# Gates read for two groups at once, twelve row sums moved from the one-hots to the second layer's groups, and three small reorderings, in a float32 transformer block pair

## The reference, cut to what matters

```
q = (xi @ w_q).reshape(n, 8, 2, 128)
s = einsum('nhpc,hpkc->nhpk', q, sub_keys)            # 128 scores on each of two sides
ts, ti = top_k(s, 16)                                 # 16 best of each side
best_s, best_p = top_k(all 256 sums of two, 16)       # 16 best pairs
gate = softmax(best_s)
act  = gelu(einsum('nd,nhkd->nhk', xi, u[idx]))
out  = einsum('nhk,nhkd->nd', gate * act, v[idx])
```

## Time and profile before

| | |
|---|---|
| time, median of 3 executions | 2229.15 us (2226.83 to 2231.83) |
| profiled execution, its own time | 2228.25 us |
| its span | 2226.9 us |
| routing (queries, key scores, u tiles, choices) | 400 to 828 us |
| one-hots | 828 to 1028 us |
| last u tiles | 1028 to about 1075 us |
| second layer's groups | about 1075 to 1590 us |
| second block | 1590 us to the end |

### The profile page before, as it was taken

One profiled execution on the slowest core, in us unless ns is written; L12 is line 12 of the kernel. 1 busy time (PEld: TensorE's weight loads), 2 busy tenths in 40 slices (PEclk: granted clock), 3 DMA queues, 4 the chain that ended last, 5 costly groups with the idle time before them and its releaser, 6 DMA issues.

```text
span 2226.9 us, 31730 instructions
## 1 busy us (share of the span) xinstructions
PE 2118.8 (95%) x12889; PEld 1230.2 (55%) x12889; DVE 1505.2 (68%) x2733; ACT 880.0 (40%) x1056; POOL 688.9 (31%) x540
## 2 busy tenths in 40 slices
PE   6999999999999989999999999999999999999998
PEld 5465665455656556666665555655645464444444
DVE  4557653798899999997788888888784374332002
ACT  5333452344334346665333333333332454434110
POOL 2421001310243332222233333334426302455440
PEclk9999999999999999999999999999999999999999
DMA  6214471215898879899999999999622201332310
GB/s 210 76 42 148 157 275 61 96 43 205 331 317 314 323 265 355 327 377 326 384 379 370 366 367 380 374 366 371 236 76 100 76 20 39 114 108 83 151 38 38
DMA packets 194482, 483.42 MB, mean 217 GB/s; under 512 B 10672, under 2 KB 93648, under 8 KB 188320
## 3 DMA queue, kind: packets, MB, share of 16 engines
q1 hardware_dynamic: 154624, 334.65, 42.0%
q0 software_dynamic: 39712, 146.74, 17.8%
HBM read 428.92 MB, written 52.43 MB: 216 GB/s over the span
## 4 chain that ended last, share of the span: by engine, by line
PE 49%; DVE 31%; DMA 13%; issue 3%; ACT 2%; POOL 1%; SPq 1%; DVEq 0%; ACTq 0%; POOLq 0%
PE psum L574 13%; PE psum L575 13%; PE psum L576 13%; DMA expert_act<-act_dram 9%; DVE weight_low L2088 7%; DVE row_sum L2336 3%; DMA rows_b<-peer_v_dram,row_index 2%; DVE rows_b L2323 2%; DVE rows_a L2323 2%; DVE hidden_low L2522 1%; POOL weight_low L2679 1%; DVE gated_one_hot_b L2502 1%; DVE one_hot_b L2499 1%; DVE one_hot_a L2496 1%; DVE expert_act L2517 1%
## 5 line engine op out<-in xcount | busy, mean ns | idle before, releaser
L574 PE MATMUL psum<-x_high,weight_high 128*128 128x384 bf16 (+3 forms) x1856 | 643.1, 346 | 16.6 <-DVE x_low L1964 5.4
L575 PE MATMUL psum<-x_low,weight_high 128*128 128x384 bf16 (+3 forms) x1856 | 642.7, 346 | 0.0
L576 PE MATMUL psum<-x_high,weight_low 128*128 128x384 bf16 (+3 forms) x1856 | 641.8, 346 | 0.0
L1348 ACT ACTIVATE weight_high<-weight_stage 128x4096 bf16<-128x4096 f32 (+2 forms) x100 | 356.2, 3563 | 260.2 <-PE psum L576 129.9
L2679 POOL TENSOR_TENSOR weight_low<-weight_stage,weight_high 128x512 bf16<-128x512 f32 (+1 forms) x229 | 296.6, 1329 | 410.4 <-ACT weight_high L1348 410.4
L574 PE MATMUL psum<-hidden_high,weight_high 128*128 128x384 bf16 x1024 | 334.5, 327 | 12.5 <-DVE hidden_low L2522 12.5
L575 PE MATMUL psum<-hidden_low,weight_high 128*128 128x384 bf16 x1024 | 334.5, 327 | 0.0
L576 PE MATMUL psum<-hidden_high,weight_low 128*128 128x384 bf16 x1024 | 334.4, 327 | 0.0
L2088 DVE TENSOR_TENSOR weight_low<-weight_stage,weight_high 128x1024 bf16<-128x1024 f32 x256 | 302.3, 1216 | 18.9 <-ACT weight_high L1348 18.8
L574 PEld LDWEIGHTS psum<-x_high,weight_high 128*128 128x128 bf16 (+1 forms) x1856 | 183.8, 99 | 169.5 <-issue 19.7
L576 PEld LDWEIGHTS psum<-x_high,weight_low 128*128 128x128 bf16 (+1 forms) x1856 | 183.8, 99 | 154.2 <-issue 6.7
(11 more groups left out here) (363 smaller groups left out, 2981.7 us busy)
## 6 DMA issues: line engine op xcount, KB each, us to landing
weight_stage<-peer_u_dram SPq DMA_DIRECT2D x32, 2048.0 KB
weight_stage<-peer_v_dram SPq DMA_DIRECT2D x32, 2048.0 KB
weight_stage<-mlp_w_dram SPq DMA_DIRECT2D x16, 2048.0 KB
weight_stage<-ada_w_dram SPq DMA_DIRECT2D x12, 2048.0 KB
act_dram<-norm_value SPq DMA_DIRECT2D x128, 192.0 KB
gate_dram<-gate_matrices SPq DMA_DIRECT2D x12, 2048.0 KB
gates<-gate_dram SPq DMA_DIRECT2D x32, 768.0 KB, 16.6
expert_act<-act_dram SPq DMA_DIRECT2D x32, 768.0 KB
```

Of the source, the lines that this page charges most:

```text
L574: self.nc.tensor.matmul(out, left[0], right[0], start=first, stop=False)
L575: self.nc.tensor.matmul(out, left[0], right[1], start=False, stop=False)
L576: return self.nc.tensor.matmul(out, left[1], right[0], start=False, stop=last)
L1348: nc.scalar.activation(k.block_view(m.w_high, n % SPLITS, n), k.block_view(m.w_stage, n % STAGES, n), ACT.Copy).then_inc(*s.w_high.up(n))
```

## The change

1. `gates` becomes twice as wide (two groups of four), and SP reads the gates of two groups in one transfer, every other group. A piece of it in memory is 1024 bytes where it was 512. The buffers are placed elsewhere so that the larger one fits.
2. `act_dram` is laid out by group, so that a group's read is one run of 6144 bytes for each partition where it was four of 1536. The 128 writes stay 128 x 1536 bytes each.
3. `ROWS_HOT` has two rows in four steps where it had three: 24 rows among the 48 steps instead of 36. `ROWS_GROUP` has 39/8 rows a group instead of 9/2, 156 instead of 144.
4. `ROUTE_ENDS` is (36, 60, 80) instead of (35, 57, 76), so 34 u tiles instead of 38 are left for the one-hots.
5. ACT's `query` takes the query first, and starts the next block's rounding one query later than before (after queries 1, 5, 9 and 13).
6. `masked` for the first two pairs comes before `small_outs` on DVE, and ACT runs one small exponential before `small_outs`.

```diff
-        m = Map(nc, top)
+        m = Map(nc, top - 512)
         self.hid_high, self.hid_low = ...
-        m = Map(nc, mats)
-        self.gates, self.act = m("gates", [P, 2, DT // TC, EG, TC]), m("expert_act", [P, 2, EG, DT])
+        self.gates = m("gates", [P, 2, DT // TC, 2 * EG, TC])
+        self.act = m("expert_act", [P, 2, EG, DT])
...
-ROUTE_ENDS = (35, 57, 76)
+ROUTE_ENDS = (36, 60, 80)
...
-ROWS_HOT = [ROWS_ROUTE[-1] + 3 * (_n + 1) // 4 for _n in range(HOT_STEPS)]
+ROWS_HOT = [ROWS_ROUTE[-1] + (_n + 1) // 2 for _n in range(HOT_STEPS)]
 ROWS_LAST = ROWS_HOT[-1] + 4
-ROWS_GROUP = [min(len(ROW_USES), ROWS_LAST + 9 * (_n + 1) // 2) for _n in range(NG)]
+ROWS_GROUP = [min(len(ROW_USES), ROWS_LAST + 39 * (_n + 1) // 8) for _n in range(NG)]
...
         def query(hp):
-            if hp % 4 == 0:
-                self.begin(("peer_q", hp // 4))
             if hp >= 2:
                 nc.scalar.wait_ge(*s.scored.at("keys", hp - 2))
             self.take(("peer_q", hp), m.query[:, hp % 2, :])
+            if hp % 4 == 1:
+                self.begin(("peer_q", hp // 4))
...
     def small_outs(self):
+        self.root_table("na", ACT.Exp)
...
         self.second_projections()
+        nc.vector.wait_ge(*s.in_window.at())
+        for p in range(2):
+            self.masked(p)
         self.small_outs()
...
-                    nc.vector.wait_ge(*s.in_gates[n % 2].at(n))
+                    nc.vector.wait_ge(*s.in_gates[n // 2 % 2].at(n // 2))
...
-            nc.sync.dma_start(k.act_dram[tile], ...)
+            nc.sync.dma_start(k.act_dram[tile // EG, :, tile % EG, :], ...)
...
         if n >= 2:
             nc.sync.wait_ge(*s.hid_low.at(n - 2, EG - 1))
-        nc.sync.dma_start(m.gates[:, n % 2, :, :, :],
-                          k.gate_dram[:, :, EG * n:EG * (n + 1), :].rearrange("c p b n -> p c b n"))...
+        if n % 2 == 0:
+            pair = n // 2
+            nc.sync.dma_start(m.gates[:, pair % 2, :, :, :],
+                              k.gate_dram[:, :, EG * n:EG * (n + 2), :].rearrange("c p b n -> p c b n"))...
-        nc.sync.dma_start(m.act[:, n % 2, :, :], k.act_dram[EG * n:EG * (n + 1)].rearrange("b p n -> p b n"))...
+        nc.sync.dma_start(m.act[:, n % 2, :, :], k.act_dram[n])...
```

More of the change, by code:

```diff
@@ L1387, in run, with root_table @@
         self.norm("final2", lambda t: s.added.at("mlp", t))
-    def root_table(self, j):
+    def root_table(self, j, func=ACT.Sqrt):
         nc, s, m = self.nc, self.s, self.m
@@ L1393, in root_table @@
             nc.scalar.wait_ge(*s.root_loaded.now())
-        nc.scalar.activation(m.root[:, 12:13], m.eps[:, 0:1], ACT.Sqrt).then_inc(*s.root_loaded.up(j))
+        nc.scalar.activation(m.root[:, 12:13], m.eps[:, 0:1], func).then_inc(*s.root_loaded.up(j))
     def norm(self, j, ready):
@@ L2514, in experts @@
                 if b == 0:
-                    nc.vector.wait_ge(*s.in_gates[n % 2].at(n))
+                    nc.vector.wait_ge(*s.in_gates[n // 2 % 2].at(n // 2))
                     nc.vector.wait_ge(*s.in_act[n % 2].at(n))
-                nc.vector.tensor_tensor(v, v, m.gates[:, n % 2, :, b, :], ALU.mult).then_inc(*s.gated.up(n, b))
+                nc.vector.tensor_tensor(v, v, m.gates[:, n // 2 % 2, :, EG * (n % 2) + b, :], ALU.mult).then_inc(*s.gated.up(n, b))
             if n < NG - 1:
@@ L2577, in small_outs, with masked @@
                                         m.x_high[:, dst + g, 0:SEQ], ALU.subtract).then_inc(*s.x_low.up(name, g))
+    def masked(self, p):
+        nc, s, m = self.nc, self.s, self.m
+        nc.vector.wait_ge(*s.in_bias[p % 2].at(p))
+        for x in range(2):
+            nc.vector.tensor_tensor(m.bias[:, p % 2, x, :, :], m.bias[:, p % 2, x, :, :], m.window[:, :, :],
+                                    ALU.add).then_inc(*s.masked.up(p, x))
     def neighbourhood(self):
         nc, s, k, m = self.nc, self.s, self.k, self.m
[L2582 to L2586, removed]
         def scores(n):
@@ L2617, in neighbourhood @@
         nc.vector.wait_ge(*s.normed.at("final1", KT - 1))
-        nc.vector.wait_ge(*s.in_window.at())
-        for p in range(2):
-            masked(p)
         n_steps = len(NA_STEPS)
@@ L2627, in neighbourhood @@
                 if t == 3 and 1 <= p < NH2 // 2 - 1:
-                    masked(p + 1)
+                    self.masked(p + 1)
                 scores(n)
@@ L2802, in fill @@
             nc.sync.wait_ge(*s.activated.at("u", tile))
-            nc.sync.dma_start(k.act_dram[tile], m.norm2.value[:, tile % 4, 0:DT]).then_inc(*s.act_spilled[tile % 4].up(tile))
+            nc.sync.dma_start(k.act_dram[tile // EG, :, tile % EG, :], m.norm2.value[:, tile % 4, 0:DT]).then_inc(*s.act_spilled[tile % 4].up(tile))
     def group(self, n):
@@ L2809, in group @@
             nc.sync.wait_ge(*s.hid_low.at(n - 2, EG - 1))
-        nc.sync.dma_start(m.gates[:, n % 2, :, :, :],
-                          k.gate_dram[:, :, EG * n:EG * (n + 1), :].rearrange("c p b n -> p c b n")).then_inc(
-            *s.in_gates[n % 2].up(n))
+        if n % 2 == 0:
+            pair = n // 2
+            nc.sync.dma_start(m.gates[:, pair % 2, :, :, :],
+                              k.gate_dram[:, :, EG * n:EG * (n + 2), :].rearrange("c p b n -> p c b n")).then_inc(
+                *s.in_gates[pair % 2].up(pair))
         for i in range(EG):
             nc.sync.wait_ge(*s.act_spilled[i].at(EG * n + i))
-        nc.sync.dma_start(m.act[:, n % 2, :, :], k.act_dram[EG * n:EG * (n + 1)].rearrange("b p n -> p b n")).then_inc(
+        nc.sync.dma_start(m.act[:, n % 2, :, :], k.act_dram[n]).then_inc(
             *s.in_act[n % 2].up(n))
@@ L2993, in build @@
     gate_dram = nc.dram_tensor("gate_dram", (DT // TC, P, NK, TC), F32, kind="Internal").ap()
-    act_dram = nc.dram_tensor("act_dram", (NK, P, DT), F32, kind="Internal").ap()
+    act_dram = nc.dram_tensor("act_dram", (NG, P, EG, DT), F32, kind="Internal").ap()
     return write(nc, dram, out, gate_dram, act_dram, reached)
```

2 lines of the change are left out of this document (1 added, 1 removed).

## The result

The changed kernel takes 2247.11 us (median of 4, 2243.23 to 2251.92), the kernel before 2227.99 on the same chip (4, 2221.72 to 2231.83). The ratio is 1.0089, interval 1.0067 to 1.0112: slower by 0.9%, where 2203 us were forecast. The profiled execution took 2251.92 us, the longest of the four, and its span is 2250.6.

What follows compares the result with a forecast made beforehand. PE was busy 95%; DVE was taken to bound the one-hots and DMA the groups. Terms -12.0 - 2.7 - 5.0 - 6.0 = -25.7 us from 2228.25 gave 2202.5, with 0.9 to the median 2203; range 2193 to 2223.

Steps and rivals of the forecast that it cites:

- Route and one-hots: From the choices to the last one-hot: twelve row passes leave DVE, which stays the bound; -12.0 us, bounds -14 and -6.
- Rival B: Among the one-hots, half of the 14 us is lost to waits and late middle picks hold DVE; 2211 us, chance 0.15.
- Queries: At the queries, ACT takes them before rounding a block, so DVE's search starts earlier; -2.7 us, bounds -3.5 and 0.
- Attention: Before attention, mask additions and table load leave the path and PE's clock stays up; -5.0 us, bounds -3.2 and -5.6.
- A drain beside the table load: Before attention, the Trainium skill adds about 1.38 us to each load; the path would lose 1.4 us more, unusable by PE.
- Groups: In the groups, fewer small DMA pieces outweigh added rows by 0.35 us a group, less longer first gates; -6 us.
- it holds by 0.7 us: In the groups, q1 never runs dry: even request 11.3 us after the last even landing, odd data landed at 12.0.
- rival C: In the groups, even activations come late, q1 runs dry in odd stretches; pair 34.7 us, time 2232.6 us, chance 0.07.
- 0.45 us a group, ... hidden by its waits for transfers: In the groups, DVE's 14 us of moved row passes return at this cost, hidden by 3.11 us of transfer waits.
- Rival A: In the groups, DMA pieces cost only their bytes, so added rows give +12 us, not -6; 2221 us, chance 0.12.
- Rival D: The groups reach PE's own pace, -13 us in place of -6; 2196 us, chance 0.10.

Runs made afterwards that it cites:

- e2: Kernel before with only the twelve row passes moved from the one-hots to the groups, four row slots: 2240.3 us, ratio 1.0075.
- e4: Kernel before with only the paired gates and the new activation layout in memory: 2232.7 us, ratio 1.0040.
- e19: Kernel before with only the new `ROUTE_ENDS` (36, 60, 80): 2229.6 us, ratio 1.0009.
- e11: Kernel before with paired gates and new activation layout, a pair's whole gates read a group earlier, behind the odd group's activations: 2216.9 us, ratio 0.9959.
- e15: Changed kernel with a pair's gates read in two halves, one a group, and a fifth slot for gathered rows: 2203.6 us, ratio 0.9882.
- e3: Changed kernel with a fifth slot for gathered rows, gates still read in one transfer a pair: 2244.3 us, ratio 1.0074.
- e17: Kernel before with the twelve rows moved to the groups and a fifth row slot: 2222.8 us, ratio 0.9991.
- e8: Kernel before with paired gates and new activation layout, but a pair's gates read in two halves, one a group: 2212.5 us, ratio 0.9949.
- e14: Changed kernel with the rows as before the change, gates read in halves and a fifth row slot: 2209.3 us, ratio 0.9905.
- e12: Changed kernel with a pair's gates read in halves, one a group, still four row slots: 2254.7 us, ratio 1.0140.

## Why the prediction was wrong

**Route and one-hots, -12.0: right.** Rows alone (e2) bring the last one-hot from 626.3 to 613.9 us after the norm, -12.4. In the change it is -11.6, and the first product -10.0. Over all profiles the last one-hot stands at 627.0 us with the rows as before (ten, 625.4 to 628.6) and at 613.0 with them moved (eight, 610.3 to 614.8): 14.0 us less, the price of the twelve passes with nothing given back. The stage took the 182 us that were forecast, picks wait 8.4 us where below 7 was said. Rival B did not come.

**Queries, -2.7: mis-sized.** ACT is free earlier, but what is late next is the transfer of the keys: PE waits 1.9 us for it, and 1.7 us at the first scores, 0.8 at the last, are left. I took ACT as the only thing that PE waited for and did not ask when `sub_keys` landed. The sum also had no term for the clock here. In five of the eight profiles without part 5 the granted clock fell behind the wait of 3.47 us, as in e2:

```profile
410.70:413.80 3.10, 3.10 (x9) 1.06 (x7) 2.48 (x13) 0.38 (x1) 3.10 (x4) 0.50 0.03 5
```

There the last key scores come 93.6 or 93.7 us behind the norm; in the other three, before, e4 and e19, the clock stayed up and they come at 92.0. With part 5 PE waits 1.9 us at most, and they come at 91.0 to 91.3 in all ten. So the term is -0.8 or, where the clock had fallen, -2.4.

**Attention, -5.0: right in this pair of traces, its bounds too narrow.** From the first scores to the end the profiles with part 6 take 455.6 or 455.7 us (nine of nine), those without it 457.3 to 457.5 (seven) or 460.1 and 460.2 (before and e11). The difference is the clock. After the same wait of 3.17 us the scores took 1.23 us in the earlier trace rows, at half clock as the earlier trace rows shows, and in e4:

```profile
1777.68 0.70 PE L1154 MATMUL psum<-na_k,na_q 64*128 64x256 f32 x4 [3.17 <-ACT na_exp L1809]
```

So the clock does not always fall after it, and the term is -1.8 or -4.5; -1.8 is outside the bounds of -3.2 and -5.6. A drain beside the table load, which the prediction weighed, is not in the trace: after the change the load of 1.28 us starts at 1786.71, 0.02 us behind the end of the instruction ahead, and the next one starts at 1788.00.

**Groups, -6.0: this is the step that failed, in two places.** The price behind it was right: 0.010 us a piece where I had 0.0119, and 12.0 to 15.3 us for twelve rows' bytes where I had 16.0. With both limits away (e15) the groups are 5.1 us shorter than before, against the -6 of the sum, and the time is 2203.6 against 2203. That the two times agree so closely is in part luck: the forecast stood on 2229.15 us for the kernel before, which took 2223.9 beside e15, so e15 wins 20.3 us by the medians (26 by the ratio) where 25.7 were forecast for the change.

First, "it holds by 0.7 us". I let the even group's request come 11.3 us behind the last even landing, the odd one land at 12.0, and 20 us of transfer follow from there, 32 for the pair. But the request finds the queue empty already. In e4 q1's last packet for an odd group ends 9.5 us behind DVE's first product of the even one (9.2 to 9.9 in 13 pairs), not 12.0, since I had worked off its 7.3 us at the mean rate of the stage. The request comes 1.35 us later, and its first packet 1.04 us behind the request, which the sum had at nothing. From the weights' issue to the landing are 1.13 + 22.39 = 23.5 and 1.16 + 20.36 = 21.5 us in e4's chain, and 21.9 to DVE's first product on the average, not 20. With 10.8 of DVE a pair takes 32.6 us from the ninth group on, and 33.2 with the first groups, not 32. The margin of 0.7 us was less than what I did not know of the rate. This is rival C, which I had given 0.07, nearly as it was drawn: the queue runs dry in the odd stretch and cannot make it up. Its price was 34.7 us a pair, and e3, where no slot binds, has 14.32 + 20.34 = 34.66. C put the late landing down to rows that crowd q1, and that is the smaller part: from the weights' issue to the first product are 22.5 us in e3 and 21.9 in e4, with the rows as before. C's time, 2232.6, still fell 12 us short of e3's, since it counted 12 pairs of 15 and nothing for the clock.

Second, the slots, which stood in no case. I wrote that DVE's rows come back as "0.45 us a group, ... hidden by its waits for transfers", and counted a row by its pass and its bytes. Its third cost is the time that its slot is taken. The trace of before had the loop in it already, with 16.5 us of DVE's waits for rows in 8 places; every second group had four rows and ended it. Going from 4 of 8 to 7 of 8 such groups took the cover away. It cost 10.3 us alone in the traces and 17.5 by the medians (e2 against e17).

Both steps also had a lower granted clock of PE behind them, for which the sum had no term on the losing side; it is 7.8 of the 34.5 us.

Rival A is excluded by the pieces' price. Rival D, PE's own pace, is reached and passed by e8 and e14, whose groups are 18.6 and 20.4 us shorter than before where D had 13; e14 has no wait of PE for `hidden_low`.

What stays open: e3 and e12 show that each limit holds the change at its level, and not how the 34.5 us of the change divide between them, since they are not added but overlap. Why e12 is slower than the change and not just as slow is not shown either.

## What to carry to other kernels

A queue that is fed on completion of what it delivered must hold more work behind each landing than the consumer needs until its next request; when transfers are paired, count that for the lighter half, and split or advance the paired one so that both halves carry the same. For transfers into a ring of slots, count how many uses per period stand against how many slots: with one more use than slots, a request slides behind the longest work of the period, and the period becomes latency plus that work. When one mend brings nothing, or makes it worse, try it beside the other before dropping it.

## What the runs showed of the hardware

Fewer and larger pieces saved 0.010 us of one DMA engine for each piece less, both from 512 to 1024 bytes (0.0099) and from 1536 to 6144 (0.0105). From the request of a transfer on the empty q1 to its first packet went 1.04 us (e4). The granted clock of PE fell to half behind one and the same idle of 3.17 us in two of nine profiles and stayed at 1.0 in the others, 2.7 us of time apart, and behind one of 3.47 us in five of eight, 1.6 us apart.
